# Triangular inverses whose first level is turned on VectorE, one modulation block moved up, and score masks put ahead of a convolution

## The reference, cut to what matters

```python
amat = jnp.where(strict, jnp.einsum('bhncd,bhnsd->bhncs', kb, k) * decay, 0.0)
rhs = jnp.concatenate([v * beta[..., None], kb * jnp.exp(gc)[..., None]], -1)
sol = lax.linalg.triangular_solve(amat, rhs, left_side=True, lower=True, unit_diagonal=True)
```

```python
sa = jnp.einsum('bhij,bhj->bhi', state, a_t)
state = state * w_t[:, :, None, :] + sa[..., None] * b_t[:, :, None, :] + v_t[..., None] * k_t[:, :, None, :]
```

## Time and profile before

| | |
|---|---|
| three runs | 2080.53, 2081.99, 2074.82 us (median 2080.53) |
| the profiled execution | 2081.45 us, of which its span is 2079.0 us |
| around the span | 2.45 us |
| granted TensorE clock, mean | 0.994 |
| TensorE busy | 2041.3 us, 98% of the span |
| VectorE busy | 1136.6 us, 55% |
| ScalarE busy | 404.5 us, 19% |
| weight loads and other reads | 290 MB from HBM, 140 GB/s over the span |

### The profile page before, as it was taken

The page is one execution under the profiler, slowest core; times in us unless marked ns, Lnnn a source line. Parts: engine busy times, 40 slices in busy tenths (PEclk is TensorE's granted clock), DMA queues, the critical chain, the costliest instruction groups (busy, mean ns, idle before and its releaser), DMA issues.

```text
span 2079.0 us, 24761 instructions
## 1 busy us (share of the span) xinstructions
PE 2041.3 (98%) x10756; PEld 1447.1 (70%) x10756; DVE 1136.6 (55%) x1618; ACT 404.5 (19%) x827; POOL 10.8 (1%) x22
## 2 busy tenths in 40 slices
PE   8999999999999999999999999999999999999998
PEld 7887765984476599446864556988884466559973
DVE  2644784755312466554344863555555764637775
ACT  2414201000121400104112642111110112321110
POOL 0000000000000000000000000000000000000000
PEclk9999999999999999999999999999999999999999
DMA  5434786444444154533231002122224453124442
GB/s 203 163 146 166 288 343 269 172 162 184 159 171 153 46 203 173 202 137 131 81 121 46 37 1 81 41 90 111 83 94 169 165 204 142 41 81 145 180 154 90
DMA packets 22747, 292.66 MB, mean 141 GB/s; under 512 B 2752, under 2 KB 3008, under 8 KB 4848
## 3 DMA queue, kind: packets, MB, share of 16 engines
q1 hardware_dynamic: 20864, 280.67, 35.7%
q0 software_dynamic: 1776, 10.43, 1.4%
HBM read 290.03 MB, written 1.05 MB: 140 GB/s over the span
## 4 chain that ended last, share of the span: by engine, by line
PE 90%; DVE 6%; DMA 3%; ACT 1%; issue 0%; SPq 0%; DVEq 0%; ACTq 0%
PE bank L325 88%; DMA ring<-in_W 2%; PE bank L686 1%; DVE small L849 1%; DVE arena L870 1%; DVE arena L863 0%; PE bank L779 0%; DMA X<-in_x 0%; DVE arena L640 0%; DVE arena L697 0%; DVE arena L844 0%; DVE HT L2459 0%; DVE arena L2587 0%; ACT arena L813 0%; ACT arena L2442 0%
## 5 line engine op out<-in xcount | busy, mean ns | idle before, releaser
L325 PE MATMUL bank<-arena 128*128 128x128 f32 (+8 forms) x3648 | 650.4, 352 | 3.4 <-DVE HT L1540 0.9
L325 PEld LDWEIGHTS bank<-arena 128*128 128x128 f32 (+3 forms) x3648 | 450.0, 183 | 187.8 <-issue 149.5
L325 PE MATMUL bank<-HT,ring 128*128 128x128 f32 (+1 forms) x2672 | 455.3, 329 | 1.7 <-DVE CP L1994 1.3
L325 PEld LDWEIGHTS bank<-HT,ring 128*128 128x128 f32 x2672 | 404.8, 191 | 47.4 <-issue 10.4
L325 PE MATMUL bank<-ring,arena 128*128 128x512 f32 (+1 forms) x674 | 295.4, 593 | 0.6 <-ACT arena L695 0.6
L325 PEld LDWEIGHTS bank<-ring,arena 128*128 128x128 f32 (+1 forms) x674 | 126.8, 190 | 156.1 <-issue 155.8
L325 PE MATMUL bank<-ring,HT 128*128 128x512 f32 (+2 forms) x512 | 192.8, 533 | 1.1 <-ACT HT L2008 0.8
L325 PE MATMUL bank<-arena,ring 128*128 128x128 f32 (+2 forms) x1046 | 172.4, 322 | 0.0
L695 ACT ACTIVATE arena<-bank 128x512 f32<-128x512 f32 (+2 forms) x133 | 72.7, 575 | 473.7 <-PE bank L325 465.4
L325 PEld LDWEIGHTS bank<-arena,ring 128*128 128x128 f32 (+1 forms) x1046 | 152.9, 191 | 13.0 <-issue 1.3
L325 PEld LDWEIGHTS bank<-ring,HT 128*128 128x128 f32 x512 | 89.5, 191 | 99.9 <-issue 95.9
(11 more groups left out here) (302 smaller groups left out, 1538.9 us busy)
## 6 DMA issues: line engine op xcount, KB each, us to landing
ring<-in_W SPq DMA_DIRECT2D x125, 2048.0 KB, 7.9
ring<-in_W SPq DMA_DIRECT2D x6, 1536.0 KB, 8.7
ring<-in_W SPq DMA_DIRECT2D x4, 1024.0 KB, 9.6
arena<-in_rel POOLq DMA_DIRECT2D x1, 2048.0 KB, 9.8
arena<-in_rpb POOLq DMA_DIRECT2D x1, 2048.0 KB, 9.3
arena<-in_dft POOLq DMA_DIRECT2D x2, 640.0 KB, 6.4
X<-in_x SPq DMA_DIRECT2D x2, 512.0 KB, 6.0
X<-in_ctx POOLq DMA_DIRECT2D x1, 1024.0 KB, 5.1
```

Source lines behind the costliest of these rows:

```text
L325: return nc.tensor.matmul(out_, lhsT, rhs, start=start, stop=stop, skip_group_check=True)
```

## The change

It has four parts. (1) `pe_inverse_first` and its ScalarE copies are gone for both inverses; `dve_inverse_first` ends with a VectorE transpose from `XT` to `XI`, and `pe_lx` waits for VectorE at level 1 too. (2) Modulation block 0 moves from behind the transposes of v to between the second half of `rkv0` and "kk wide", in the plan ahead of `rkv2`; every later modulation block moves up by one place, and the last place that is left empty is the second one of chunk step c = 0. (3) `pe_scores("mrb")` moves ahead of the half of `bqkv0`, and the masks of "mrb" and "mrk" ahead of `dve_conv(0)`. (4) The final modulation product of the first half (`pe_mod(0)`, `dve_mod(0)`) moves from level k = 2 to k = 1 of the delta rule's inverse, since its last block is now one place earlier.

```diff
 def weight_plan():
-    plan += [("lora_in", 8 * 256), ("rkv1", 4096), ("rkv0", 4096), ("lora_out", 3 * 512), ("rkv2", 4096)]
+    plan += [("lora_in", 8 * 256), ("rkv1", 4096), ("rkv0", 4096), ("lora_out", 3 * 512), ("ada0.0", 4096), ("rkv2", 4096)]
     ada = [(f"ada{j // 12}.{j % 12}", 4096) for j in range(24)]
-    plan += [ada[0], ("bqkv0", 4096), ada[1], ("bqkv1", 4096), ada[2], ("bqkv2", 4096), ada[3], ("bgate", 4096), ada[4], ("bab", 64)] + ada[5:]
+    plan += [ada[1], ("bqkv0", 4096), ada[2], ("bqkv1", 4096), ada[3], ("bqkv2", 4096), ada[4], ("bgate", 4096), ada[5], ("bab", 64)] + ada[6:]
...
-        def pe_inverse_first(label, groups, XT):
-            for g in range(groups):
-                pe.wait_ge(vector_done, at(f"{label} 1.{g} X"))
-                pe_turn(f"{label} first{g}", [XT[:, 4 * g + i, :] for i in range(4)])
...
-            if k == 1:
-                pe.wait_ge(scalar_done, at(f"read {label} first{g}"))
-            else:
-                pe.wait_ge(vector_done, at(lab + " X"))
+            pe.wait_ge(vector_done, at(lab + " X"))
...
-        def dve_inverse_first(label, g, LT, XT):
+        def dve_inverse_first(label, g, LT, XT, XI):
...
             tt(XT[:, s, :], XT[:, s, :], rows(K("ident"), 4), ALU.add).then_inc(vector_done, dve.one())
+            dve.wait_ge(vector_done, dve.n)
+            src, dst = (v[:, s, :].rearrange("p a c -> p (a c)") for v in (XT, XI))
+            nc.vector.transpose(dst, src).then_inc(vector_done, dve.one())
             dve.mark(f"{label} 1.{g} X")
...
             pe_half_block("rkv0", "raw r", 1, 0)
+            pe_ada(0)
             pe.wait_ge(vector_done, at("kk inv"))
...
-            pe_ada(0)
+            pe_ada(1)
+            pe_scores("mrb", AV, R)
             pe_half_block("bqkv0", "bq", 0, 0)
-            pe_inverse_first("rwkv", 4, XT1)
-            pe_scores("mrb", AV, R)
             pe_scores("mrk", KF, R)
...
-            pe_ada(9)
+            pe_ada(10)
             pe_chunk_out(0)
-            pe_inverse_first("gdn", 2, XT2)
-            pe_ada(10)
+            pe_ada(11)
...
-                if k == 2:
+                if k == 1:
                     pe_mod(0)
...
-                pe_ada((18, 20, 22, 23)[c])
+                pe_ada((19, 20, 22, 23)[c])
                 pe_bchunk_out(c)
-                if c < 2:
-                    pe_ada(19 + 2 * c)
+                if c == 1:
+                    pe_ada(21)
...
-            for g in range(4):
-                copy_out(act, f"rwkv first{g}", XI1[:, 4 * g:4 * g + 4, :], lambda ps: k4(ps[:, :]))
...
-            for g in range(2):
-                copy_out(act, f"gdn first{g}", XI2[:, 4 * g:4 * g + 4, :], lambda ps: k4(ps[:, :]))
...
             stt(KF, TMP, 1.0, KF, ALU.add, ALU.mult).then_inc(vector_done, dve.one())
+            dve_ada(0)
             for g in range(4):
                 ps = full(dve, f"kk wide{g}")
...
-            dve_ada(0)
-            dve_conv(0)
+            dve_ada(1)
             dve_mask("mrb", MRB, "upto")
             dve_mask("mrk", MRK, "upto")
+            dve_conv(0)
...
                 if k == 1:
+                    dve_mod(0)
                     tt(QK, QK, rows(K("upto"), 8), ALU.mult).then_inc(vector_done, dve.one())
...
                     tt(k42(KBP), k8, wide(BEG), ALU.mult).then_inc(vector_done, dve.one())
-                    dve_mod(0)
```

More of the change, by code:

```diff
@@ L1309, in pe_mix @@
                 pe.mark(f"lv{t}")
-            pe_ada(1)
+            pe_ada(2)
             for k in range(1, 6):
@@ L1321, in pe_mix @@
                 else:
-                    pe_ada(6)
+                    pe_ada(7)
                     pe_bnorm_spread()
@@ L1330, in pe_mix @@
                 if k < 5:
-                    pe_ada(k + 1)
-            pe_ada(7, banks["rwkv 5.0 XLXt"])
-            pe_ada(8, banks["rwkv 5.1 XLXt"])
+                    pe_ada(k + 2)
+            pe_ada(8, banks["rwkv 5.0 XLXt"])
+            pe_ada(9, banks["rwkv 5.1 XLXt"])
             for t in range(2):
@@ L1361, in pe_mix @@
                 else:
-                    pe_ada(2 * k + 6)
+                    pe_ada(2 * k + 7)
                 for g in range(2):
                     pe_xlx("gdn", k, g, LX2, XT2)
-                if k == 2:
+                if k == 1:
                     pe_mod(0)
@@ L1368, in pe_mix @@
                     pe_chunk_out(k)
-                    pe_ada(10 + k)
+                    pe_ada(11 + k)
                 else:
-                    pe_ada(2 * k + 7)
+                    pe_ada(2 * k + 8)
             pe.wait_ge(vector_done, at("gdn ready"))
@@ L1706, in dve_mix @@
             for g in range(4):
-                dve_inverse_first("rwkv", g, LT1, XT1)
+                dve_inverse_first("rwkv", g, LT1, XT1, XI1)
             dve_mask("lak", LAK, "before")
             dve.mark("lak ready")
-            dve_ada(0)
-            dve_conv(0)
+            dve_ada(1)
             dve_mask("mrb", MRB, "upto")
             dve_mask("mrk", MRK, "upto")
+            dve_conv(0)
             dve.wait_ge(tensor_done, at("lv1"))
@@ L1716, in dve_mix @@
                 dve_masked("rwkv", 1, g, MASKED1, LT1)
-            dve_ada(1)
+            dve_ada(2)
             for k in range(1, 6):
@@ L1740, in dve_mix @@
                 if k == 5:
-                    dve_ada(6)
+                    dve_ada(7)
                 if k < 5:
@@ L1754, in dve_mix @@
                 if k < 5:
-                    dve_ada(k + 1)
+                    dve_ada(k + 2)
             for c in range(4):
@@ L1762, in dve_mix @@
             dve.mark("bqk normed")
-            dve_ada(7)
             dve_ada(8)
+            dve_ada(9)
             dve.wait_ge(scalar_done, at("lv out"))
@@ L1789, in dve_mix @@
             for g in range(2):
-                dve_inverse_first("gdn", g, LT2, XT2)
+                dve_inverse_first("gdn", g, LT2, XT2, XI2)
             for t in range(2):
@@ L1797, in dve_mix @@
                 dve_masked("gdn", 1, g, MASKED2, LT2)
-            dve_ada(9)
+            dve_ada(10)
             dve_chunk_out(0)
-            dve_ada(10)
+            dve_ada(11)
             dve.wait_ge(scalar_done, at("gcb exp"))
@@ L1820, in dve_mix @@
                 else:
-                    dve_ada(2 * k + 6)
+                    dve_ada(2 * k + 7)
                 for g in range(2):
@@ L1830, in dve_mix @@
                     dve_chunk_out(k)
-                    dve_ada(10 + k)
+                    dve_ada(11 + k)
                 else:
-                    dve_ada(2 * k + 7)
+                    dve_ada(2 * k + 8)
                 if k == 1:
+                    dve_mod(0)
                     tt(QK, QK, rows(K("upto"), 8), ALU.mult).then_inc(vector_done, dve.one())
@@ L1857, in dve_mix @@
                     dve_y_out()
-                dve_ada((18, 20, 22, 23)[c])
+                dve_ada((19, 20, 22, 23)[c])
                 dve_bchunk_out(c)
-                if c < 2:
-                    dve_ada(19 + 2 * c)
+                if c == 1:
+                    dve_ada(21)
                 if c == 0:
```

## The result

Over 20 runs each the kernel before has a median of 2080.76 us and the changed one 2083.47 us; the ratio changed to before is 1.0022, 95% interval 1.0013 to 1.0030. The change makes the kernel slower by 0.1 to 0.3%, less than the 0.3% that was taken as the bound of no change, and inside the range. The changed kernel's profiled execution took 2083.63 us, its span 2081.8. Between the two profiled executions the difference is +2.2 us.

What follows compares the result with a forecast made beforehand. TensorE, busy 98% of the span, was taken as the bound, the weight stream from 299 us. Terms 7.7 - 1.2 - 4.0 = +2.5, plus 1.7 for the clock, put 2081.45 at 2085.7 us; range 2079 to 2091.

Steps and rivals of the forecast that it cites:

- Transposes off TensorE: In the RWKV and delta rule's inverses, sixteen and eight transposes leave TensorE's path: -2.9 us.
- The block ahead of `rkv2`: At `rkv2`, its load now waits for `rkv0`'s slot; TensorE idles 5.7 us, everything after is 7.63 us late.
- "mrb": Ahead of the "mrb" scores, TensorE waits for banks the "lak" masks free: +2.9 us; the convolution's 0.9 us wait goes.
- The clock: Idle time lowers TensorE's clock: +1.7 us at the start of `rkv2`, 0 at the hole ahead of "mrb".
- rival 1: Clock falls in both holes, at `rkv2` and the half of `bqkv0` behind "mrb": 5.1 us, total 2089.1 us; chance 0.37.
- a second low stretch after 97: Sign in the clock after 97 us, behind the hole ahead of "mrb", that would make it rival 1.
- rival 3: Around "lv", the old low-clock stretch from 103.3 to 113.4 goes: -5 us, total 2080.7 us; chance 0.08.
- The three rivals about the clock: At the holes and "lv": rival 1 (0.37), no fall in either hole (2084.0 us, 0.06), and rival 3 (0.08).
- The delta rule's inverse: At its first levels, modulation block 11 and a chunk step hide VectorE's added transposes; sum -1.2 us, -1.0 already counted.
- The chunk steps: One block less: 1.85 us and 3.4 us of block waits go, VectorE's lateness adds 1.2; sum -4.0 us.

Runs made afterwards that it cites:

- the turns alone: Kernel before with part 1 of the change only (first-level transposes on VectorE, order of everything else as before): 2080.32 us, ratio 0.9993.
- the block-behind kernel: Changed kernel with modulation block 0 behind `rkv2` instead of ahead of it, in the plan too: 2077.69 us, ratio 0.9984.
- the fill: Changed kernel with 38 matmuls into an unread bank put into the idle time ahead of `rkv2`: 2086.02 us, ratio 1.0026.
- the second trace: Kernel before, unchanged, run and profiled once more: median 2081.3 us, ratio 1.0006 against itself, profiled execution 2073.4 us.
- both repairs: Changed kernel with modulation block 0 behind `rkv2` and the "lak" masks between the groups of the first level: 2074.91 us, ratio 0.9972.
- the bank edit: Rotating bank counter raised by 6 at the stage's end, on top of both repairs and "bonus" ahead of "mrb": 2072.54 us, ratio 0.9970.

## Why the prediction was right

The forecast was +4.2 us and no change that can be measured; the medians say +2.7, the ratio +4.6 and the two profiled executions, for which the sum was made, +2.2. The waits were foreseen; of the three changes in the clock the forecast had one, mis-sized. That the number came so near is in part luck: two terms of the clock of nearly 5 us each cancelled in this execution, and of the 2.9 us by which the stage itself came out below the forecast (1.3 at its end instead of 4.2), 0.9 were lost again behind it. By its steps:

- **Transposes off TensorE**, -2.9: they are gone, and the earlier trace rows gave their price; the turns alone confirm that up to 130 us nothing waits for VectorE in their place. Their worth in the time is less than the sum says: that kernel gained 0.8 us, within the noise, and a later wait takes some of it back.
- **The block ahead of `rkv2`**: the load landed after 7.6 us, not 8.1, and the hole is 5.2 us, not 5.7. The mechanism and its size were right, and the block-behind kernel shows that this one place costs 5.8 us.
- **"mrb"**: a wait of 2.65 us against 2.7, ended by the masks of "lak" as counted from the banks. The convolution's wait is gone.
- **The clock**: mis-sized, in both signs. `rkv2` lost 2.9 us (16.9 against 14.0 with the fill), where 1.7 was taken from the start of the trace; in two other traces with this hole it lost 1.7 and 1.5. At the second hole I took 0, and it cost 1.6: "mrb" 3.38 against 2.06, the half projection 7.44 against 7.17; of the five traces with this hole, four have the fall. So rival 1's two falls came, at 4.5 us where it said 5.1, and by my own sign, a second low stretch after 97, this was rival 1 and not the forecast. But rival 3 came too in this execution: "lv", the block behind it and the start of level 1 had lost 2.4, 1.7 and 0.7 us before, and lost nothing now. (I had put 3.1 on "lv" from a row that mixes two shapes; the whole, 4.8 against 5, was right.) The clock thus changed the sum by -0.3 and not by +1.7. The three rivals about the clock are not alternatives; each fall happens or not by itself, and I should have priced them as independent terms.
- **The delta rule's inverse**: from 6.5 us late to 4.9 at level 5, -1.6 against -1.2. The cover was just enough: no wait for VectorE over 0.15 us there, nor at the mask.
- **Not in the sum**: between 195 and 225 us the loss of clock behind the last small projection was smaller than before, and TensorE waited 1.8 us for a block instead of 0.35. Here weights are the bound, and what TensorE gains ahead of it is handed back. Both kept the shift at 6.5.
- **The chunk steps**: -3.6 against -4.0. The waits for blocks went from 3.4 to 0.5, and VectorE was late by 0.3, 0.5 and 0.9 where 0.4, 0.3 and 0.5 were counted. This is what part 2 brings, and it is kept by the version that puts the block behind `rkv2`.
- **Behind the stage**: I counted nothing there, and the bank counter cost 1.1 us, the slower landing of the store 0.8; 0.6 came back around the span.

The two traces add up: the block 1.85, the first hole with its clock 8.1, the second 4.3 (2.7 in the starts, 1.6 of clock), the convolution -0.9, transposes -1.9, the loss at "lv" that did not recur -4.8: +6.7, as measured behind it (123.02 against 116.35). Then -0.2, -1.6 and -3.6 lead to the 1.3 behind the chunk steps. By execution, the two terms of the clock, +4.5 and -4.8, come and go.

## What to carry to other kernels

A block moved in a ring of weights is moved for the loads too: look up whose release its successors now wait for, before asking whether the engine has time for it. With three slots, one block of little work (1.85 us) between two projections made the load of the second start only when the first was used up; one place later the moved block cost 5.8 us less. And a rotating buffer counter ties all stages together: opening fewer banks in one stage changes who waits in the next.

## What the runs showed of the hardware

**The clock makes the groups of run times.** Of the 79 runs of the kernel before that were taken beside the experiments, nine lie below 2075 us, and their mean granted clock is 0.997 or 0.998; the other 70, from 2077.2 up to 2089.7, have 0.990 to 0.996. So the fast group is one of fewer or shorter low stretches. The four of 20 runs near 2074 us in the comparison above are the size of an execution without the low stretch at "lv" (the second trace: 2073.4); that it is this stretch that is missing from them rests on the two profiled executions. The Trainium skill (TensorE: Matmul & The Clock Gate, "HAM oscillation") says that waits between bursts bring the low clock back; the two holes agree with it (0.50 behind each). But the clock also fell with no idle time ahead, while TensorE was busy with "lv" (64 columns) right behind "bonus" (2 columns). The kernel with both repairs shows this; its TensorE has no wait between 55 and 130 us:

```profile
98.26 2.06 PE L325 MATMUL bank<-arena 64*128 64x128 f32 x32
100.25 1.95 PE L325 MATMUL bank<-KC,arena 128*128 128x2 f32 x16
102.05 4.87 PE L325 MATMUL bank<-arena 128*128 128x64 f32 x32
106.85 3.64 PE L325 MATMUL bank<-ring,SCW 128*32 128x512 f32 x16
```

"lv" takes 4.87 us instead of 3.76 and the block behind it 3.64 instead of 1.92. Whether it falls differs from execution to execution of one program.

**Work that computes nothing can pay.** With 22 dummy matmuls in a hole of 5.2 us the median was 1.7 us lower, at the edge of what these runs can tell, and in the trace the projection behind the hole ran at full clock.

**What stays open.** How often each fall of the clock comes was not measured beyond these traces. The early "mrb" (part 3) and the earlier modulation product (part 4) were not run by themselves. A bank offset that spares both the later stages and the end of this one was not looked for. The fastest version, 2073.0 us and 0.3 to 0.4% below the kernel before (2072.5 with the bank edit), has the turns on VectorE, block 0 behind `rkv2`, the masks of "lak" between the groups, and "bonus" ahead of "mrb".
